# Attention values in eight batches, paired output statistics, doubled low and compressed buffers, and gates in the batches' steps

## The reference, cut to what matters

```python
(hq, hf_, hi, hg, nq, kc, vc, ksl, vsl, kwn, vwn, ngate, gate_a, gate_b) = split(rms_norm(x) @ w_in)
y_a = hgrn2_mixer(hq, hf_, hi, hg, lb, out_gain) @ w_branch_a
y_b = nsa_mixer(nq, ...) @ w_branch_b
x = x + (sigmoid(gate_a) * y_a + sigmoid(gate_b) * y_b) @ w_out
x = x + square(relu(rms_norm(x) @ w_up)) @ w_down
# hgrn2: scores[t, s] = sum_d q[t,d] k[s,d] decay(s..t, d);  o = scores @ v;  rms_norm per head of 128, times silu(g)
# nsa, per block of 128 queries: compressed, selected and sliding-window attention, 8 heads of 64 in 2 groups
s_c = q_b @ k_cmp * scale + bias;  p_c = masked_softmax(s_c);  o_c = p_c @ v_cmp
s_s = q_b @ k_sel * scale + bias;  o_s = masked_softmax(s_s) @ v_sel
s_w = q_b @ k_win * scale + bias;  o_w = masked_softmax(s_w) @ v_win
out = gate0 * o_c + gate1 * o_s + gate2 * o_w
```

## Time and profile before

| | us |
|---|---|
| median of 3 runs | 794.11 |
| lowest, highest | 793.34, 794.18 |
| the profiled execution | 794.33 |
| its span | 792.6 |
| TensorE busy | 784.2 |
| VectorE busy | 410.4 |
| ScalarE busy | 216.2 |
| GpSimd busy | 489.7 |

### The profile page before, as it was taken

How to read it: one execution, slowest core, us unless ns; L and a number is a source line. 1 busy time by engine, 2 the same in 40 slices (tenths; PEclk the granted TensorE clock), 3 DMA queues, 4 the chain that set the end, 5 groups by cost and what they waited for, 6 DMA issues and landing times.

```text
span 792.6 us, 12362 instructions
## 1 busy us (share of the span) xinstructions
PE 784.2 (99%) x4604; PEld 639.1 (81%) x4604; DVE 410.4 (52%) x580; ACT 216.2 (27%) x436; POOL 489.7 (62%) x325
## 2 busy tenths in 40 slices
PE   8999999999999999999999999999999999999998
PEld 6788878888777787778888888888888888888886
DVE  4795488946566565725467666660000567640000
ACT  6200754356422555733122222210000122210000
POOL 4666645677455756656666666766666667666563
PEclk9999999999999999999999999999999999999999
DMA  8244221233522011034223232232232322323320
GB/s 282 81 143 171 87 82 62 75 133 107 186 73 87 28 39 44 2 106 160 88 98 106 81 106 82 103 106 85 101 105 80 107 90 96 106 91 121 132 79 26
DMA packets 23548, 77.99 MB, mean 98 GB/s; under 512 B 2723, under 2 KB 3499, under 8 KB 23380
## 3 DMA queue, kind: packets, MB, share of 16 engines
q1 hardware_dynamic: 19964, 69.00, 25.9%
q10 hardware_dynamic: 3544, 8.44, 3.0%
HBM read 75.31 MB, written 4.21 MB: 100 GB/s over the span
## 4 chain that ended last, share of the span: by engine, by line
PE 94%; DVE 3%; DMA 1%; POOL 1%; issue 0%; SPq 0%; ACT 0%; DVEq 0%; POOLq 0%
PE bank L413 26%; PE bank L415 26%; PE bank L414 26%; PE bank L752 2%; PE bank L797 2%; PE bank L785 2%; PE bank L507 1%; PE bank L508 1%; PE bank L509 1%; DMA x<-in_xT 1%; PE bank L556 1%; POOL wsp L333 1%; PE bank L437 1%; PE bank L668 1%; DVE pc L1522 1%; DVE tot L1328 0%
## 5 line engine op out<-in xcount | busy, mean ns | idle before, releaser
L333 POOL TENSOR_TENSOR wsp<-wraw,wsp 128x1024 fp32r<-128x1024 f32 x124 | 305.8, 2466 | 10.4
L331 POOL TENSOR_SCALAR wsp<-wraw 128x1024 fp32r<-128x1024 f32 x124 | 135.9, 1096 | 237.4 <-PE bank L415 153.0
L413 PE MATMUL bank<-hhi,wsp 128*128 128x512 f32 x352 | 141.4, 402 | 1.8 <-DVE hlo L1239 1.2
L415 PE MATMUL bank<-hhi,wsp 128*128 128x512 f32 x352 | 137.3, 390 | 0.0
L414 PE MATMUL bank<-hlo,wsp 128*128 128x512 f32 x352 | 137.2, 390 | 0.0
L413 PE MATMUL bank<-ghi,wsp 128*128 128x512 f32 x256 | 100.4, 392 | 0.0
L415 PE MATMUL bank<-ghi,wsp 128*128 128x512 f32 x256 | 99.7, 390 | 0.0
L413 PE MATMUL bank<-uhi,wsp 128*128 128x512 f32 x256 | 99.7, 389 | 0.0
L414 PE MATMUL bank<-glo,wsp 128*128 128x512 f32 x256 | 99.6, 389 | 0.0
L414 PE MATMUL bank<-ulo,wsp 128*128 128x512 f32 x256 | 99.6, 389 | 0.0
L415 PE MATMUL bank<-uhi,wsp 128*128 128x512 f32 x256 | 99.6, 389 | 0.0
(11 more groups left out here) (271 smaller groups left out, 1052.9 us busy)
## 6 DMA issues: line engine op xcount, KB each, us to landing
wraw<-in_w SPq DMA_DIRECT2D x126, 512.0 KB, 3.3
bias_skewed<-bias_lines ACTq DMA_DIRECT2D x1, 2048.0 KB
bias<-bias_skewed ACTq DMA_DIRECT2D x1, 2048.0 KB, 8.9
x<-in_xT ACTq DMA_DIRECT2D x1, 2048.0 KB, 9.4
out<-x ACTq DMA_DIRECT2D x8, 256.0 KB, 2.0
x<-in_xT SPq DMA_DIRECT2D x3, 512.0 KB, 7.5
x<-in_xT SPq DMA_DIRECT2D x2, 256.0 KB, 5.0
wraw<-in_w SPq DMA_DIRECT2D x4, 128.0 KB, 8.4
```

Source lines behind the costliest of these rows:

```text
L331: pool.tensor_scalar(whi[:, two, :], wraw[:, raw, :], 1.0, 0.0, ALU.mult, ALU.add).then_inc(w_hi, 1)
L333: pool.tensor_tensor(wlo[:, two, :], wraw[:, raw, :], whi[:, two, :].bitcast(F32), ALU.subtract).then_inc(w_split, 1)
L413: pe.matmul(out_, wh, mh, start=first, stop=False)
L415: return pe.matmul(out_, wl, mh, start=False, stop=last)
```

## The change

- **Values.** `values(gi, 0)` and `values(gi, 1)` now follow each other, behind `turn` in steps 7, 11, 15 to 35. `pt_low` has two buffers, so that the low half of group gi is evacuated while that of group gi - 1 may still be read; the waits of `evacuate` are set to that.
- **Projections and gates of b.** gb3, gb4, gb5 and gb6 are made in steps 8, 12, 20 and 28 (before 7, 13, 19, 30), gates in steps 7, 11, 15, 23 and 31 (before 5, 9, 15, 21, 31). gb7's eight parts are cut 3, 3, 2.
- **Reciprocals.** The fourth tile of each group is inverted at the end of its own step, not in the middle of the next.
- **Output statistics.** Two heads at a time, each with 64 columns of ones into one half of bank 6, behind ga0 and ga2. ScalarE makes both inverse roots together and writes them to both halves of the partitions.
- **Level 64.** Blocks with odd t go to the other half of the partitions; one bank, one `keep_64` for all heads. Level 128 takes the pairs in the order 1, 0. Two head norms and the one before them move behind `keep_64`.
- **advance.** The totals of the next level are made behind the products of this one.
- **Compressed scores.** Two buffers `pc`; VectorE makes block qb + 1 ahead of the gate that stands behind block qb.

```diff
-GB_AFTER = {3: "gb2", 7: "gb3", 13: "gb4", 19: "gb5", 30: "gb6", 33: "gb7"}
-GATE_AT = {5: "gb2", 9: "gb3", 15: "gb4", 21: "gb5", 31: "gb6"}
-GB7_AT = {32: (0, 2), 33: (2, 6), 34: (6, 8)}
+GB_AFTER = {3: "gb2", 8: "gb3", 12: "gb4", 20: "gb5", 28: "gb6", 33: "gb7"}
+GATE_AT = {7: "gb2", 11: "gb3", 15: "gb4", 23: "gb5", 31: "gb6"}
+GB7_AT = {32: (0, 3), 33: (3, 6), 34: (6, 8)}
...
-        pt_low = at("pt_low", 186.5, [P, 2, 2, 256])
+        pt_low = [at("pt_low0", 186.5, [P, 2, 2, 256]), at("pt_low1", 160.5, [P, 2, 2, 256])]
...
-        pc = at("pc", 177, [P, 256])
+        pc = [at("pc0", 177, [P, 256]), at("pc1", 202.5, [P, 256])]
...
             def level_64():
                 pe.wait_ge(decayed, 7)
-                for pair in range(2):
-                    to = sc_bank()
-                    for h in (2 * pair, 2 * pair + 1):
-                        for t in range(ST):
-                            c = (h % 2) * 256 + t * 64
-                            last = pe.matmul(to[0:64, c:c + 64], k_dec[:, h, t * P:t * P + 64],
-                                             q_dec[:, h, t * P + 64:t * P + P], start=True, stop=True)
-                    last.then_inc(sc_done, 1)
+                to = sc_bank()
+                for h in range(HG):
+                    for t in range(ST):
+                        c, r0 = h * P + t // 2 * 64, t % 2 * 64
+                        last = pe.matmul(to[r0:r0 + 64, c:c + 64], k_dec[:, h, t * P:t * P + 64],
+                                         q_dec[:, h, t * P + 64:t * P + P], start=True, stop=True,
+                                         skip_group_check=True)
+                        if h == HG - 1 and t >= 2:
+                            last.then_inc(sc_done, 1)
...
-            def output_stat(h):
+            def output_stats(pair):
                 pe.wait_ge(part_lo, PART["kw"] + 1)
-                pe.wait_ge(pair_read, 4 + h)
-                stat(f"st_o{h}", ones[:], sq[:, h % 2, :], to=bank[6])
+                pe.wait_ge(pair_read, 4 + pair)
+                pe.wait_ge(stat_in, stats[0] + 2)
+                stats[0] += 2
+                for n in range(2):
+                    pe.matmul(bank[6][64 * n:64 * n + 64, :], ones[:, 0:64], sq[:, n, :], start=True, stop=True,
+                              skip_group_check=True).then_inc(stat_out, 1)
...
-            for h in range(1, HG):
-                project(f"ga{h}")
-                output_stat(h)
-
+            project("ga1")
+            project("ga2")
+            output_stats(1)
+            project("ga3")
...
-                done = t - VALUES
-                if done >= 8 and done % 8 == 1:
-                    pe.wait_ge(cv_placed, done // 8)
-                    values(done // 4, 0)
                 if LAG <= t < NT + LAG:
                     turn(t - LAG)
-                if done >= 0 and done % 2 == 0 and (done == 0 or done % 8):
-                    values(done // 4, done // 2 % 2)
+                if t >= VALUES + 2 and (t - VALUES - 2) % 4 == 0:
+                    gi = (t - VALUES - 2) // 4
+                    if gi and gi % 2 == 0:
+                        pe.wait_ge(cv_placed, gi // 2)
+                    values(gi, 0)
+                    values(gi, 1)
...
+            def inverse_rms_of_two():
+                outs[0] += 2
+                act.wait_ge(stat_out, outs[0])
+                link(act.activation(tmp[:], bank[6][:], ACT.Ln, scale=1.0 / P, bias=eps))
+                act.sem_inc(pair_read, 1)
+                act.wait_ge(rs_used, rs[0])
+                for n in range(2):
+                    rows = slice(64 * n, 64 * n + 64)
+                    act.activation(rstd[0:64, n, :], tmp[rows, :], ACT.Exp, scale=-0.5)
+                    act.activation(rstd[64:128, n, :], tmp[rows, :], ACT.Exp, scale=-0.5).then_inc(rs_ready, 1)
+                rs[0] += 2
...
-                if gi >= 1:
-                    act.wait_ge(pv_done[0], 2 * (gi - 1) + qb // 2 + 1)
-                to = (pt_low, pt_high)[qb // 2]
+                if gi >= 2 - qb // 2:
+                    act.wait_ge(pv_done[0], (2 * gi - 3, 2 * gi)[qb // 2])
+                to = (pt_low[gi % 2], pt_high)[qb // 2]
...
-                dve.tensor_tensor(totals(2 * m).rearrange("p (n one) -> p n one", one=1), t[:, :, 0:1], t[:, :, 1:2],
-                                  ALU.mult)
                 dve.tensor_tensor(kv[:, :, 0, :], kv[:, :, 0, :], t[:, :, 1:2].broadcast_to([P, nb, m]), ALU.mult)
...
                 dve.sem_inc(decayed, 1)
+                last = dve.tensor_tensor(totals(2 * m).rearrange("p (n one) -> p n one", one=1), t[:, :, 0:1], t[:, :, 1:2],
+                                         ALU.mult)
...
             gate("ga4")
+            c_shift(0)
+            c_weight(0)
             for qb in range(ST):
-                c_shift(qb)
-                c_weight(qb)
+                if qb + 1 < ST:
+                    c_shift(qb + 1)
+                    c_weight(qb + 1)
                 gate(("ga5", "ga6", "ga7", "gb0")[qb])
...
-                if 2 <= t <= NT and t - 1 not in GB_AFTER:
+                if 2 <= t <= NT and t - 1 not in GB_AFTER and (t - 1) % 4 < 3:
                     invert(t - 1)
...
-                if t in GB_AFTER and t < NT:
+                if t < NT and (t in GB_AFTER or t % 4 == 3):
                     invert(t)
```

More of the change, by code:

```diff
@@ L599, in level_256 @@
                 for h in range(HG):
-                    to = sc_bank() if h < 2 else bank[h]
+                    if h < 2:
+                        pe.wait_ge(sc_kept[h], (6, 5)[h])
+                    to = bank[6 + h if h < 2 else h]
                     for j in range(2):
@@ L734, in c_turn @@
                 for g in range(2):
-                    last = pe.transpose(bank[4][:, g * P:g * P + P], pc[:, g * P:g * P + P], ident[:])
+                    last = pe.transpose(bank[4][:, g * P:g * P + P], pc[qb % 2][:, g * P:g * P + P],
+                                        ident[:])
                 last.then_inc(cpT_done, 1)
@@ L790, in values @@
                 i, b = divmod(gi, 2)
-                pt = (pt_low, pt_high)[half]
+                pt = (pt_low[gi % 2], pt_high)[half]
                 for g in range(2):
@@ L1028, in _ @@
             inverse_rms("st_q3", DH)
-            for n in range(2):
-                act.wait_ge(sc_done, SC_128 + n + 1)
+            for n in (1, 0):
+                act.wait_ge(sc_done, SC_128 + 2 - n)
                 act.activation(sc[:, 2 * n:2 * n + 2, 4:6, :].rearrange("p h b t -> p h (b t)"),
@@ L1117, in _, with out_of_head @@
+            def out_of_head(h):
                 act.wait_ge(oa_f, h + 1)
                 act.activation(oahi[:, h, :], o_ring[:, h % 2, :], ACT.Copy).then_inc(oa_hi, 1)
-                if h == 0:
-                    act.wait_ge(skew_out, 16)
-                    act.dma_start(bias[:], skewed.rearrange("h p u -> p h u")).then_inc(bias_in, 16)
-            for qb in range(ST):
+            inverse_rms_of_two()
+            square_o(2)
+            square_o(3)
+            key_low_again("ks")
@@ new lines, in _, with c_exp @@
+            key_low_again("kw")
+            out_of_head(0)
+            act.wait_ge(skew_out, 16)
+            act.dma_start(bias[:], skewed.rearrange("h p u -> p h u")).then_inc(bias_in, 16)
+            out_of_head(1)
+            inverse_rms_of_two()
+            out_of_head(2)
+            act.wait_ge(cst_done, 1)
+            for g in range(2):
+                act.activation(pcT[g][:], cst_bank[g][:], ACT.Copy).then_inc(cst_kept, 1)
+            out_of_head(3)
+            def c_exp(qb):
@@ L1124, in _ @@
                 act.wait_ge(cs_shift, qb + 1)
                 nc_ = 8 * qb + 7
-                pcv = pc[:].rearrange("p (h c) -> p h c", h=NH)[:, :, 0:nc_]
+                pcv = pc[qb % 2][:].rearrange("p (h c) -> p h c", h=NH)[:, :, 0:nc_]
                 act.activation(pcv, pcv, ACT.Exp, scale=-1.0).then_inc(cp_ready, 1)
+            c_exp(0)
+            c_exp(1)
+            for qb in range(ST):
                 act.wait_ge(cpT_done, qb + 1)
@@ L1349, in keep_64 @@
             def keep_64():
-                for pair in range(2):
-                    dve.tensor_copy(sc[0:64, 2 * pair:2 * pair + 2, 0:4, 64:P],
-                                    bank[6 + pair][0:64, :].rearrange("p (h t c) -> p h t c", h=2, t=4)
-                                    ).then_inc(sc_kept[pair], 1)
+                for odd in range(2):
+                    last = dve.tensor_copy(
+                        sc[0:64, :, odd:4:2, 64:P],
+                        bank[6][64 * odd:64 * odd + 64, :].rearrange("p (h t c) -> p h t c", h=HG, t=2))
+                last.then_inc(sc_kept[0], 1)
             normed_n = [0]
@@ L1498, in _ @@
             oa_low(HG - 1)
-            link(dve.memset(pc[:], 0.0))
+            for two in range(2):
+                link(dve.memset(pc[two][:], 0.0))
             def by_head(v):
```

41 lines of the change are left out of this document (18 added, 23 removed).

## The result

The changed kernel takes **787.95 us** (median of 6 runs, 787.08 to 788.34) against 794.11 (6 runs, 793.34 to 794.18): a ratio of 0.9924, 95% interval 0.9911 to 0.9937, 6.2 us less. The profiled execution took 787.78 us, with a span of 786.0, against 794.33 and 792.6. In a later job the same kernel gave 787.34 against 793.6, ratio 0.992.

A forecast was written before the change was run, and what follows sets the result against it. The prediction took TensorE's own list of instructions, busy 784.2 of 792.6 us, plus few waits as the bound. Its terms summed to -6.1 us, from 794.3 to 788.2 us, range 786.0 to 790.9.

The forecast's parts named there:

- Batches of values: Attention loop: 16 blocks of values become 8 batches, each block costing 0.35 us of switching; -2.8 us.
- Waits that go: Attention loop: TensorE's wait for GpSimd's scaling goes, -1.05 us, and five smaller waits at transposes, -0.55 us.
- Waits that come: Attention loop: transposes wait for VectorE's copy of 512 columns, seven cycles at 0.17; +1.2 us, bounds 0 and 2.9.
- Decay levels: Level 64's alternating column halves overlap, -0.95 us; an earlier signal removes the wait ahead of level 2, -0.35 us.
- Statistics: Output statistics among projections: two heads paired in column halves, twice instead of four times; -1.15 us, bounds -1.7 and +0.4.
- Compressed scores: Two buffers make each block one projection ahead, removing waits before transpositions; -0.45 us, bounds 0 and -0.6.
- (a): Rival: VectorE absorbs everything, no new waits in the loop; -7.3 us, 787.0 us; chance 0.22.
- (b): Rival: loop waits near their bound or beyond, 3 to 4 us instead of 1.2; 790.5 us; chance 0.22.
- (c): Rival: column halves don't overlap; levels give back 0.95, statistics 1.55; 790.7 us; chance 0.05.
- (d): Rival: gates in batches' steps delay each cycle's first tile, 1.4 us a cycle; slower, 796.8 us; chance 0.03.

The follow-up runs named there:

- the loop's part alone: The kernel before with only the changed kernel's batches, second low buffer, gate tables and reciprocal places; statistics, decay levels and compressed scores as before: 790.68 us.
- the repeated experiment: The changed kernel with decay level 64 in one half of the columns again, each of its two banks waited for only when used: 788.44 us.
- 1.12 in the undo: The changed kernel with one full-width statistics matmul for each head in place of the two paired half-width ones: 788.95 us.
- 0.59 in the undo: The changed kernel with one buffer of compressed scores' weights instead of two, and the engines' order of before there: 788.12 us.

## Why the prediction held, point by point

The forecast was 788.2 us, in a range of 786.0 to 790.9; the median is 787.95. Its sum of -6.1 us stands against -5.98 in the traces behind the start. That the profiled executions differ by 6.55 is half a microsecond of the start, which no term forecast; the 788.2 was also reckoned from the profiled execution, 0.2 above the median.

- **Batches of values, -2.8.** Right in size between the two kernels. Without the block, transposes and scores are 0.60 + 0.79 = 1.39 us (forecast 1.38), and 24 values in one go are 2.31, that is 0.64 more than the 16 alone (forecast 0.65). So one block cost 2.38 - 1.39 - 0.64 = 0.35 us. The price belongs to a place, though: between scores of 512 columns and two transposes an extra block cost 0.28. The gaps from a last matmul's start to the start of what follows show why. Behind six transposes, which stand 0.03 to 0.11 us apart, the first value comes 0.20 later; behind scores of 512 columns, 0.23 apart anyway, 0.33 later, so only 0.1 more. A switch seems to cost what is left of the last matmul, and behind a long one most of that passes anyway; no run here varied that length alone. The mode itself has a price: in the changed kernel's trace the last matmul of a projection stands 0.32 or 0.33 us ahead of what follows in all 14 places where that is in another mode than 128*128, and 0.23 in all 20 where the mode stays. The Trainium skill, "TensorEngine Tiling (Array Packing)", section Tiling Modes, Key Properties, says that a change of tiling mode drains TensorE and a change of tile within a mode doesn't. These rows agree, and so does level 64, whose tiles change at every matmul with instructions 0.03 us apart.
- **Waits that go, -1.05 and -0.55.** They went, in the changed kernel and in the one with the loop's part alone. That the steps of projections and gates keep the loop free of such waits is shown by the run with the tables of before: with the batches and the old steps there are five waits of 0.9 us, where the kernel before had one. Which part of the change removed the old wait itself (steps, reciprocals or the second buffer) wasn't run apart. That the old steps would do so much harm I had not worked out; the prediction needed only that the new ones leave none.
- **Waits that come, +1.2.** Seven cycles lost 0.15 to 0.21 us each in the transposes of tile 4k, 1.29 in all, and 0.2 more stood in four smaller places. The mechanism named was the one found: VectorE's 512-column copy (319.20 for 0.69 us), and the batch put ahead removed it in six cycles of seven.
- **Decay levels, -0.95 and -0.35.** 0.93 and 0.36, both shown by the traces, the first also by the repeated experiment; no run undid the order of the totals. The 0.1 I allowed for a wait ahead of level 128 came the other way: the gap there fell from 0.33 to 0.13 us, while levels 128 and 256 took 0.05 and 0.10 more.
- **Statistics, -1.15.** 1.13 in the trace, 1.12 in the undo. The row of the compressed values (1.15 for two passes) was a good stand-in: the pair takes 1.01, with its two edges of 0.1 it costs 1.20.
- **Compressed scores, -0.45.** Mis-sized: 0.56 over the stretch, 0.59 in the undo. The two late starts were 0.25 and 0.21 us, as forecast. What I missed is inside the transpositions: the second of each pair waits too, 0.05 us in three of them, because the earlier trace rows were read for the start only.
- **The rivals.** (a) lay 1 us below the median and fell with the waits that came. (b), 3 to 4 us of new waits, is what comes if the batches meet the tables of before, 4.7. (c) fell: 32 matmuls of level 64 in 1.08 us. (d), the kernel slower than before, didn't come; with the tables of before its mechanism, GpSimd's scaling late for the first tile of a cycle, appears with 0.9 us of idle time in three cycles, but not in all seven.

## What to carry to other kernels

On an engine that is busy 99% of the time, look at the gaps between starts where one form of work follows another: the same instructions gathered into fewer blocks gave 2.8 us here, at 0.28 to 0.35 a block, more behind the short transposes than behind scores of 512 columns. When one engine's blocks are moved, the order on its partners is part of the change: the same batches with the steps of before for gates and projections were 4.8 us slower, and their loop 1.7 us slower than with no batches at all, and half a batch moved without its evacuations brought 1.5 us of new waits. And an undo must give back the waits as they were, not only the work; a bank asked for too early cost 0.8 us and looked like a larger effect.

## What was not expected of the hardware

**VectorE and GpSimd hold each other up.** GpSimd's product of 1024 columns takes 2.4 us by itself and VectorE's with two operands in SBUF 1.2. In the changed kernel, first GpSimd's and VectorE's timelines around 97 us, then those around 134 us:

```profile
97.15 2.41 POOL L333 TENSOR_TENSOR wsp<-wraw,wsp 128x1024 fp32r<-128x1024 f32 x1
...
97.18 3.46 DVE L1359 TENSOR_TENSOR k_dec<-k_dec,f 128x1024 f32<-128x1024 f32 x1 [0.60 <-PE bank L556]
100.57 1.21 DVE L1360 TENSOR_TENSOR q_dec<-q_dec,f 128x1024 f32<-128x1024 f32 x1
...
133.56 3.40 POOL L333 TENSOR_TENSOR wsp<-wraw,wsp 128x1024 fp32r<-128x1024 f32 x1
...
133.47 1.23 DVE L1359 TENSOR_TENSOR k_dec<-k_dec,tot 128x1024 f32<-128x1024 f32 x1 [0.48 <-PE bank L570]
134.62 3.42 DVE L1360 TENSOR_TENSOR q_dec<-q_dec,tot 128x1024 f32<-128x1024 f32 x1
```

Whoever starts second is longer by what is left of the other: 3.46 is 2.4 and then 1.1 of its own; at 133.56 GpSimd waits first (3.40), and then VectorE's second product does (3.42). The Trainium skill, "SBUF — State Buffer", section Who interferes with whom, says that such a VectorE instruction contends with a GpSimd one that reads SBUF, and that the port pair they share is an exclusive lock; the rows agree. Here it delays the signal that level 2 waits for; moving the totals behind the two products brought that signal forward, and TensorE had use for 0.36 us of it. No run here tried to keep the two apart.

**A pause costs more than itself.** The first matmul behind a wait has 0.34 us to the next start where its pace is 0.23 (scores of tile 3, with and without the wait). In the tables' run a wait shown as 0.91 us idle made a gap of 1.18 between two transposes whose pace is 0.11, so it cost 1.07. The 0.34 isn't the pause's alone: behind a block of transposes, with no pause, a projection's first matmul has 0.31 to the next start.
